# Two attention stages: both heads of a pair turned back to back, weighed values gathered in one PSUM bank

## The chip, the cores and the metric

The kernel runs on one core of a Trainium2 chip, as one program with one launch. The metric is the device time of that program in microseconds, and a version is described by the median of several executions. Abbreviations: PE is TensorE (PEld its weight loads), DVE is VectorE, ACT is ScalarE, POOL is GpSimd, SP is SyncE, which starts most transfers.

## The reference

Two model blocks over a sequence of 2048 rows of width 1024, batch 1, in float32. Only two pieces of them are touched here, the attentions, each with 8 query heads of width 64:

```python
# first block: window of 128 keys to either side, 2 key/value heads, one sink logit per query head
scores = jnp.einsum('bnqhgd,bnkhd->bnhgqk', qb, kb) * (SWA_HEAD_DIM ** -0.5)
scores = jnp.where(valid, scores, -jnp.inf)
mx = jnp.maximum(jnp.max(scores, axis=-1, keepdims=True), sink)
p = jnp.exp(scores - mx)
denom = jnp.sum(p, axis=-1, keepdims=True) + jnp.exp(sink - mx)
out = jnp.einsum('bnhgqk,bnkhd->bnqhgd', p / denom, vb)
...
# second block: chunks of 64 queries, each with its own chunk and the 8 chunks left of it, 8 key/value heads
scores = jnp.where(valid, scores * scale + bias, NEG_BIG)
p = jax.nn.softmax(scores, axis=-1)
out = jnp.einsum('bhcqk,bkhd->bcqhd', p, vb)
```

Around them stand projections, a gated delta rule, a convolution branch, norms and output products. They are not changed.

## The kernel before

The program is a chain of stages, each with its own tiles and semaphores; a stage begins when the one ahead of it has ended. Both attentions are one function, `attention`, called with the name `wa` (window attention, first block) and `ca` (chunk attention, second block). The names of tiles carry this prefix.

**Tiling.** The queries come in 16 tiles of 128 rows. The 8 heads are 4 pairs (m = 0 to 3), the two heads of a pair (g = 0, 1) lie in the upper and the lower 64 partitions. So there are 64 pairs in each attention, two pairs make a half, and a tile has two halves. A query tile sees n key tiles of 128 keys: in `wa` 3 (2 in the first and the last tile), in `ca` 5 (1, 2, 3, 4 in the first four tiles).

**Steps of a pair.**
- Scores (L2013, PE): n key tiles against one query tile, 64 rows deep, the two heads in the two halves of the array at once. Result in `s`, one buffer for each head.
- Maximum (L2131, DVE, for each head): adds bias or mask, negates, takes the row's minimum, writes `neg` (one buffer for each head).
- Exponent (L2192, ACT, for each head): writes `pr` (two rounds of buffers) and the row's sum.
- Turning (L2024, PE, for each head): n transposes of 128x128 with the whole array. Result in `t`, two banks, one buffer that both heads share in turn.
- Copy of what was turned (L2200, ACT, for each head): `t` to `prt`.
- Values (L2038, PE): 2n products with 64 output columns, the two heads in the two column halves of the array. Result in the first half of `o`, one bank for each half of the tile.

**Steps of a half.** Denominators (L2083 with sinks, L2086, L2089, DVE) give `rden`; the spread (L2047, PE) turns it into the second half of the same `o` bank with two whole-array transposes; the copy of the spread (L2211, ACT) brings it to `rd`; finish (L2097, in `ca` also L2103 with the gate, DVE) multiplies the values with it. Once a tile, ACT starts the store (L2216), and in `ca` the load of the gates (L2232).

**Order.** It is written out by hand for each engine. On PE, in the round of pair m: scores(m), turn(m-1, head 0), values(m-2), turn(m-1, head 1), and behind a half's second pair its spread. The array is used in three ways: split by rows (scores), whole (turning, spread), split by columns (values). ACT goes copy(m-1, 0), exponent(m, 0), copy(m-1, 1), exponent(m, 1), with the copy of a spread ahead of the first. DVE goes maximum(m, 0), maximum(m, 1), with finish and denominators behind the second one. Turn(m-1, 1) waits until head 0's turned tile has been copied, since they share `t`. In `wa`, DVE and ACT also split weights for the stage behind it (L2165, L2248) from the eighth tile on.

Of the kernel before, what the change touches and what calls it, by code (L numbers as in the profile page):

```python
# [27 lines left out]
F32 = mybir.dt.float32  # L28
# [7 lines left out]
P = 128  # L36
# [1821 lines left out]
def attention(nc, name, warm, n_warm, consts, load_tile, n_kt, bias_of, bias_shape, load_bias, sink_rows, lanes, shapes, span, out,  # L1858
# [8 lines left out]
    PAIRS = 4  # L1867
    with Ctx(nc, name, USED) as c:
# [6 lines left out]
        neg = [c.sb(f"neg{g}", [P, n_kt * P]) for g in G]  # L1875
        pr = [[c.sb(f"pr{r}{g}", [P, n_kt * P]) for g in G] for r in S]
        prt = [[c.sb(f"prt{r}{g}", [P, n_kt * P]) for g in G] for r in S]
# [7 lines left out]
        s_ps = [c.ps(f"s{g}", [P, bank]) for g in G]  # L1885
        t_ps = c.ps("t", [P, 1024])
        o_ps = [c.ps(f"o{half}", [P, 4, P]) for half in S]
# [3 lines left out]
        scored = c.sems("scored", 2)  # L1891
        max_done = c.sems("max_done", 2)
        exp_done = c.sems("exp_done", 2)
        turned = c.sems("turned", 2)
        pt_copied = c.sems("pt_copied", 2)
        weighed = c.sems("weighed", 2)
# [46 lines left out]
        def program(tile, flush):  # L1943

            for t in range(TILES):
                tile(span_of(t - 1) if t else None, span_of(t))
            flush(span_of(TILES - 1))

        def lagged(before, now, m, lag):

            return (now, m - lag) if m >= lag else (before, m - lag + PAIRS)
# [45 lines left out]
        @block.tensor  # L1997
        def _(pe):
            keep_warm(nc, t_ps[:, 0:NCOL], warm, n_warm)
            pe.wait_ge(const_in, 16 * n_const + START)  # L2000

            def scores(now, m):
                t, u, s, lo, n, b0 = now
                M = PAIRS * t + m
                if m == 0:
                    pe.wait_ge(tile_in, LD * 16 * min(TILES, t + ahead + 1) + START)
                for g in G:
                    wait(pe, max_done[g], M)
                for a in range(0, n * P, 512):
                    w = min(512, n * P - a)  # L2010
                    for g in G:
                        rows = slice(HD * g, HD * g + HD)
                        mm = nc.tensor.matmul(s_ps[g][:, a:a + w], qr[rows, m, t * P:(t + 1) * P],  # L2013
                                              kr[rows, key_tile(m), lo * P + a:lo * P + a + w], start=True, stop=True)
                        if a + w == n * P:
                            mm.then_inc(scored[g], 1)

            def turn(now, m, g):
                t, u, s, lo, n, b0 = now
                M = PAIRS * t + m  # L2020
                pe.wait_ge(exp_done[g], M + 1 + START)
                wait(pe, pt_copied[1 - g], M + g)
                for a in range(n):
                    mm = nc.tensor.transpose(t_ps[:, a * P:(a + 1) * P], pr[m % 2][g][:, a * P:(a + 1) * P], ident[:])  # L2024
                mm.then_inc(turned[g], 1)

            def values(now, m):
                t, u, s, lo, n, b0 = now
                M = PAIRS * t + m
                half = m // 2  # L2030
                for g in G:
                    pe.wait_ge(pt_copied[g], M + 1 + START)
                if m % 2 == 0:
                    wait(pe, half_done[half], t)
                for a in range(n):
                    for g in G:
                        v0 = value_at(m, g)
                        mm = nc.tensor.matmul(o_ps[half][HD * g:HD * g + HD, m % 2, :], vr[:, lo + a, v0:v0 + HD],  # L2038
                                              prt[m % 2][g][:, a * P:(a + 1) * P], start=(a == 0), stop=(a == n - 1))
                        if a == n - 1:  # L2040
                            mm.then_inc(weighed[g], 1)
# [20 lines left out]
            def tile(before, now):  # L2062
                for m in range(PAIRS):
                    scores(now, m)
                    behind(before, now, m)

            def flush(last):
                behind(last, None, 0)
                values(last, PAIRS - 1)
                spread(last, 1)  # L2070

            program(tile, flush)

        @block.vector
        def _(dve):
            def denominators(now, half):
                t, u, s, lo, n, b0 = now
                at = slice(4 * half, 4 * half + 4)
                for g in G:
                    dve.wait_ge(exp_done[g], PAIRS * t + 2 * half + 2 + START)  # L2080
# [11 lines left out]
            def finish(now, half):  # L2092
                t, u, s, lo, n, b0 = now
                dve.wait_ge(rd_copied[half], t + 1 + START)
                if half == 0:
                    wait(dve, stored[s], 16 * u)
                nc.vector.tensor_tensor(ob[s][:, 2 * half:2 * half + 2, :], o_ps[half][:, 0:2, :], rd[half][:],  # L2097
# [11 lines left out]
            def sink_minus_max(now, half):  # L2109
                t, u, s, lo, n, b0 = now  # L2110
                at = slice(4 * half, 4 * half + 4)
                for g in G:
                    dve.wait_ge(max_done[g], PAIRS * t + 2 * half + 2 + START)
# [3 lines left out]
            def tile(before, now):  # L2117
                t, u, s, lo, n, b0 = now
                for m in range(PAIRS):
                    if before is None and not sinks:  # L2120
                        dve.wait_ge(bias_in[m], 16 + START)
                        pair = slice(2 * m, 2 * m + 2)
                        nc.vector.tensor_scalar(bias[:, pair, :], bias[:, pair, :], 1.0 / scale, None, ALU.mult).then_inc(
                            scaled, 1)
                        dve.wait_ge(scaled, m + 1 + START)
                    for g in G:
                        h = 2 * m + g
                        M = PAIRS * t + m
                        dve.wait_ge(scored[g], M + 1 + START)
                        wait(dve, exp_done[g], M)  # L2130
                        nc.vector.tensor_tensor_reduce(neg[g][:, 0:n * P], s_ps[g][:, 0:n * P],  # L2131
                                                       bias_of(bias, h)[:, b0:b0 + n * P], -scale,
                                                       sink[:, 1, h:h + 1] if sinks else HUGE, ALU.add, ALU.min,
                                                       nmx[s][:, h:h + 1]).then_inc(max_done[g], 1)
                        if h == 1 and before:
                            finish(before, 0)
                            denominators(before, 1)
                        if h == 3 and sinks:
                            sink_minus_max(now, 0)
                        if h == 5:  # L2140
                            denominators(now, 0)
                        if merge and t == 13 and h == 2:
                            dve.wait_ge(merge_hi, 1 + START)
                            nc.vector.tensor_tensor(merge.wlo[:], merge.raw[:], merge.whi[:].bitcast(F32),
                                                    ALU.subtract).then_inc(merge_lo, 1)
                        if h == 7 and before:
                            finish(before, 1)
                        if h == 7 and sinks:
                            sink_minus_max(now, 1)
                        if later and t in (2, 3) and h == 4:  # L2150
# [1545 lines left out]
```

## Time and profile before

| | |
|---|---|
| median of 3 runs | 3193.09 us (3183.62 to 3195.11) |
| profiled execution | 3180.22 us, its span 3178.4 us |
| TensorE busy, share of the span | 2981.4 us, 94% |
| VectorE busy | 1791.1 us, 56% |
| ScalarE busy | 1296.3 us, 41% |
| granted TensorE clock, mean | 0.97 |
| `wa`, first turning to last step | 1145.3 to about 1323 us |
| `ca`, first turning to last step | 2555.8 to about 2795 us |

Busy times are of one profiled execution. A matmul's end is modelled, so PE's starts say more than its ends: the distance from the start of one group to the start of the next is what a step costs on PE. In the timeline, rows that belong together are merged (x5 is five instructions), and the brackets at the end give the idle time ahead of a row with what ended it; "issue" means that the profile shows no engine that was waited for.

### The profile page before, as it was taken

To read this page: it belongs to the slowest core of one execution; us is meant where nothing else is said; L and a number is where in the kernel's file an instruction comes from. 1 tells how busy PE (TensorE), PEld (TensorE's weight loads), DVE (VectorE), ACT (ScalarE), POOL (GpSimd) and SP (SyncE) were. 2 spreads that over 40 slices of the span, in tenths; PEclk is the share of its full clock that TensorE was granted. 3 is DMA by queue.
4 is the path that set the end of the run, shared out by engine and by line. 5 is a ranking of instruction groups with operands and counts; after the bars stand their busy time and mean duration, and the time that the engine had idled before them with its cause. 6 is when DMAs were issued, how large, how long until landed. Compare 5 with 4: busy or idle time off the path is not lost. (4 is left out here: it accounts for less than half of the span.)

```text
span 3178.4 us, 56341 instructions
## 1 busy us (share of the span) xinstructions
PE 2981.4 (94%) x21262; PEld 2410.2 (76%) x21262; DVE 1791.1 (56%) x3269; ACT 1296.3 (41%) x2704; POOL 551.5 (17%) x475
## 2 busy tenths in 40 slices
PE   7998999998999989899789999999999989989998
PEld 6886998775888856578468888878888757768787
DVE  5755443074777746655565785565776445553433
ACT  5222433154665558611433323433323367730132
POOL 0000000062343400032022232342233100000000
PEclk9999999999999989999899999999999989999999
DMA  4222775153554432255633223453223263145443
GB/s 140 80 80 75 246 256 195 52 159 134 182 184 151 139 112 94 81 191 186 216 104 106 86 67 103 141 164 107 73 70 106 91 207 115 34 151 213 172 145 119
DMA packets 288037, 423.39 MB, mean 133 GB/s; under 512 B 41520, under 2 KB 178736, under 8 KB 282160
## 3 DMA queue, kind: packets, MB, share of 16 engines
q1 hardware_dynamic: 239312, 383.87, 35.8%
q10 hardware_dynamic: 48480, 36.18, 3.6%
q8 instruction: 162, 2.65, 0.3%
q14 instruction: 83, 0.68, 0.1%
HBM read 270.56 MB, written 149.42 MB: 132 GB/s over the span
## 5 line engine op out<-in xcount | busy, mean ns | idle before, releaser
L114 PE MATMUL pj_pp<-h_hi,pj_whi 128*128 128x512 f32 x1152 | 449.6, 390 | 5.7 <-POOL h_lo L3086 5.7
L116 PE MATMUL pj_pp<-h_hi,pj_wlo 128*128 128x512 f32 x1152 | 448.8, 390 | 0.0
L115 PE MATMUL pj_pp<-h_lo,pj_whi 128*128 128x512 f32 x1152 | 448.7, 389 | 0.0
L114 PEld LDWEIGHTS pj_pp<-h_hi,pj_whi 128*128 128x128 f32 x1152 | 216.4, 188 | 52.1 <-issue 7.6
L2913 ACT CAST pj_whi<-w_raw 128x512 fp32r<-128x512 f32 x192 | 119.5, 624 | 325.6 <-PE pj_pp L116 313.5
L115 PEld LDWEIGHTS pj_pp<-h_lo,pj_whi 128*128 128x128 f32 x1152 | 216.5, 188 | 44.9
L116 PEld LDWEIGHTS pj_pp<-h_hi,pj_wlo 128*128 128x128 f32 x1152 | 216.5, 188 | 44.9
L2977 DVE TENSOR_TENSOR pj_wlo<-w_raw,pj_whi 128x512 fp32r<-128x512 f32 x192 | 161.2, 840 | 12.1 <-ACT pj_whi L2913 8.8
L114 PE MATMUL np_pp<-h_hi,np_whi 128*128 128x512 f32 x384 | 150.4, 392 | 0.0
L115 PE MATMUL np_pp<-h_lo,np_whi 128*128 128x512 f32 x384 | 149.8, 390 | 0.0
L116 PE MATMUL np_pp<-h_hi,np_wlo 128*128 128x512 f32 x384 | 149.7, 390 | 0.0
L2131 DVE CUSTOM_DVE_ANT_0 ca_neg<-ca_s,ca_bias 128x640 f32<-128x640 f32 (+4 forms) x128 | 90.0, 739 | 101.8 <-PE ca_s L2013 100.9
L3106 POOL TENSOR_TENSOR w_raw<-w_raw,pj_t 128x512 f32<-128x512 f32 x48 | 62.7, 1307 | 438.9 <-DVE pj_wlo L2977 438.9
L2913 ACT CAST pj_whi<-pj_t 128x512 fp32r<-128x512 f32 x96 | 59.9, 624 | 173.7 <-PE pj_pp L116 152.2
L1669 POOL TENSOR_TENSOR gr_sw<-gr_tab,gr_wrow 128x64 f32<-128x64 f32 x32 | 15.8, 521 | 642.7 <-DMA gr_ident<-in_consts 642.7
L345 DVE SCALAR_TENSOR_TENSOR np_acc<-np_pre,np_taps,np_acc 128x2048 f32<-128x2048 f32 (+3 forms) x60 | 115.5, 1926 | 2.1
L114 PE MATMUL mo_pp<-ahead_whi,mo_mhi 128*128 128x512 f32 x256 | 103.4, 404 | 0.0
L115 PE MATMUL mo_pp<-ahead_wlo,mo_mhi 128*128 128x512 f32 x256 | 101.8, 398 | 0.0
L116 PE MATMUL mo_pp<-ahead_whi,mo_mlo 128*128 128x512 f32 x256 | 101.8, 397 | 0.0
L2200 ACT COPY ca_prt<-ca_t 128x640 f32<-128x640 f32 (+4 forms) x128 | 80.2, 627 | 51.8 <-PE ca_t L2024 51.2
L114 PE MATMUL fo_pp<-fo_whi,fo_mhi 128*128 128x512 f32 x256 | 99.8, 390 | 0.0
L115 PE MATMUL fo_pp<-fo_wlo,fo_mhi 128*128 128x512 f32 x256 | 99.6, 389 | 0.0
(411 smaller groups left out, 7228.5 us busy)
## 6 DMA issues: line engine op xcount, KB each, us to landing
w_raw<-in_w_second SPq DMA_DIRECT2D x192, 256.0 KB, 2.9
ds_pk<-scratch_pack SPq DMA_DIRECT2D x32, 1280.0 KB, 7.5
scratch_pack<-rp_out SPq DMA_DIRECT2D x32, 512.0 KB, 2.7
scratch_sig_fm<-pj_ob SPq DMA_DIRECT2D x64, 256.0 KB, 2.1
mb_sg<-scratch_sig_fm SPq DMA_DIRECT2D x16, 1024.0 KB, 7.2
rp_fm<-scratch_qkv_fm SPq DMA_DIRECT2D x96, 128.0 KB, 2.9
scratch_qkv_fm<-np_acc SPq DMA_DIRECT2D x11, 1024.0 KB, 4.8
np_acc<-in_x SPq DMA_DIRECT2D x16, 512.0 KB, 4.3
```

What stands on the lines that cost most here:

```text
L114: nc.tensor.matmul(out, ah, bh, start=(first and i == 0), stop=False)
L115: nc.tensor.matmul(out, ah, bl, start=False, stop=False)
L116: mm = nc.tensor.matmul(out, al, bh, start=False, stop=(last and i == n - 1))
L345: nc.vector.scalar_tensor_tensor(out=acc[s][:, at], in0=pre[s][:, at.start + t:at.stop + t], scalar=taps[:, n, t:t + 1], in1=acc[s][:, at] ...
L1669: ins = nc.gpsimd.tensor_tensor(sw[s][:, :, k, a:a + HH], tab[s][:, 1, :, a:a + HH], wrow[:, k, b:b + HH].unsqueeze(1).to_broadcast([P, 2, ...
L2131: nc.vector.tensor_tensor_reduce(neg[g][:, 0:n * P], s_ps[g][:, 0:n * P], bias_of(bias, h)[:, b0:b0 + n * P], -scale, sink[:, 1, h:h + 1] ...
L2200: nc.scalar.copy(prt[m % 2][g][:, 0:n * P], t_ps[:, 0:n * P]).then_inc(pt_copied[g], 1)
L2913: nc.scalar.copy(whi[i], raw_of[i]).then_inc(hi_ready[i], 1)
L2977: nc.vector.tensor_tensor(wlo[i], raw_of[i], whi[i].bitcast(F32), ALU.subtract).then_inc(lo_ready[i], 1)
L3106: nc.gpsimd.tensor_tensor(raw[1][0], raw[1][0], t2[:], ALU.subtract).then_inc(t4_ready, 1)
```

## The change

In both attentions:
- `t` becomes three tiles of one bank each: one for each head, which holds up to four turned key tiles, and a third for the fifth key tile of both heads (`ca` only).
- The two heads of a pair are turned back to back (then, in `ca`, the fifth key tiles of both), and the values of the pair before come behind them. PE's round is scores, spread, turns, values. ACT copies 4 key tiles for each head, and in `ca` with one more instruction the fifth ones of both heads (`copy_last`).
- `o` shrinks to one bank. Values and spread of both halves share it, so there are new waits on PE: the second pair's values of a half wait for the copy of that half's spread (`rd_copied`), and the first pair's values and the spread wait until the other half has been finished (`half_done`). The spread is issued ahead of its half's last values, no longer behind them.
- ACT goes exponent(q, 0), copy of the spread, copy(q-1, 0), exponent(q, 1), copy(q-1, 1), `copy_last`. DVE has finish ahead of the maxima, denominators behind them. The gates' load stands at the head of a tile with a wait of its own, the store one pair earlier.

The new code can take one or two pairs a round (`deep`); both calls pass `deep` = 1, so below SLOTS is (0, 1), GROUPS_OF is 4, NQ is 64, HALF_OF is 2, and q counts pairs.

```diff
-        t_ps = c.ps("t", [P, 1024])
-        o_ps = [c.ps(f"o{half}", [P, 4, P]) for half in S]
+        t_ps = [c.ps(f"t{b}", [P, 4, P]) for b in range(3)]
+        o_ps = c.ps("o", [P, 4, P])
...
+        def half_ending(q):
+
+            return (span_of(q // GROUPS_OF), (q % GROUPS_OF) // HALF_OF) if 0 <= q < NQ and (q + 1) % HALF_OF == 0 else None
...
+            def turns(q):
+                (t, u, s, lo, n, b0), m0 = group(q)
+                for k in SLOTS:
+                    pe.wait_ge(exp_done[k], q + 1 + START)
+                    q1, k1 = bank_before(q, k)
+                    wait(pe, pt_copied[k1], q1 + 1)
+                    for a in range(min(n, 4)):
+                        mm = nc.tensor.transpose(t_ps[bank_of(q, k)][:, a, :], pr[q % 2][k][:, a * P:(a + 1) * P], ident[:])
+                    mm.then_inc(turned[k], 1)
+                if n > 4:
+                    wait(pe, last_copied, last_tiles(q) - 1)
+                    for k in SLOTS:
+                        mm = nc.tensor.transpose(t_ps[2][:, k, :], pr[q % 2][k][:, 4 * P:5 * P], ident[:])
+                    mm.then_inc(last_turned, 1)
+
+            def values(q):
+                (t, u, s, lo, n, b0), m0 = group(q)
+                half = m0 // 2
+                if half_ending(q):
+                    pe.wait_ge(rd_copied[half], t + 1 + START)
+                if m0 % 2 == 0:
+                    wait(pe, half_done[1 - half], t + half)
+                if n > 4:
+                    pe.wait_ge(last_copied, last_tiles(q) + START)
...
             def spread(now, half):
                 t, u, s, lo, n, b0 = now
                 pe.wait_ge(den_inv[half], t + 1 + START)
+                wait(pe, half_done[1 - half], t + half)
                 for r in range(2):
-                    mm = nc.tensor.transpose(o_ps[half][:, 2 + r, :], rden[half][:, r, :], ident[:])
+                    mm = nc.tensor.transpose(o_ps[:, 2 + r, :], rden[half][:, r, :], ident[:])
                 mm.then_inc(spread_done[half], 1)
 
-            def behind(before, now, m):
-                t1, m1 = lagged(before, now, m, 1)
-                t2, m2 = lagged(before, now, m, 2)
-                if t1:
-                    turn(t1, m1, 0)
-                if t2:
-                    values(t2, m2)
-                if t1:
-                    turn(t1, m1, 1)
-                if t2 and m2 % 2:
-                    spread(t2, m2 // 2)
...
+            for q in range(NQ + 2):
+                if q < NQ:
+                    scores(q)
+                if half_ending(q - 2):
+                    spread(*half_ending(q - 2))
+                if 1 <= q <= NQ:
+                    turns(q - 1)
+                if q >= 2:
+                    values(q - 2)
...
             def finish(now, half):
                 t, u, s, lo, n, b0 = now
                 dve.wait_ge(rd_copied[half], t + 1 + START)
+                for k in SLOTS:
+                    dve.wait_ge(weighed[k], (GROUPS_OF * t + HALF_OF * (half + 1)) + START)
...
+            for q in range(NQ + 3):
+                if q < GROUPS_OF and not sinks:
+                    scale_bias(q)
+                if half_ending(q - 3):
+                    finish(*half_ending(q - 3))
+                for k in SLOTS:
+                    if q < NQ:
+                        add_and_max(q, k)
+                    if k == 1 and half_ending(q - 1):
+                        denominators(*half_ending(q - 1))
+                    if q < NQ:
+                        beside(q // GROUPS_OF, 2 * deep * (q % GROUPS_OF) + k)
+                if sinks and half_ending(q):
+                    sink_minus_max(*half_ending(q))
...
+            def copy_last(q):
+                act.wait_ge(last_turned, last_tiles(q) + START)
+                for k in SLOTS:
+                    wait(act, weighed[k], q - 1)
+                nc.scalar.copy(prt[q % 2][:, :, 4 * P:5 * P], t_ps[2][:, 0:2 * deep, :]).then_inc(last_copied, 1)
...
+            for q in range(NQ + 3):
+                if q < NQ and q % GROUPS_OF == 0 and gb is not None:
+                    load_gates(q // GROUPS_OF)
+                for k in SLOTS:
+                    if q < NQ:
+                        exponent(q, k)
+                    if k == 0 and half_ending(q - 2):
+                        copy_spread(*half_ending(q - 2))
+                    if 1 <= q <= NQ:
+                        copy_turned(q - 1, k)
+                    if q < NQ:
+                        beside(q // GROUPS_OF, 2 * deep * (q % GROUPS_OF) + k)
+                if 1 <= q <= NQ and last_tiles(q - 1) > last_tiles(q - 2):
+                    copy_last(q - 1)
+                if sinks and half_ending(q):
+                    sink_exponent(*half_ending(q))
+                if half_ending(q - 3) and half_ending(q - 3)[1]:
+                    store(half_ending(q - 3)[0])
```

## Rows read from the trace of the kernel before

**Rows 1.** Windows: busy time and count by engine, granted clock, DMA share, GB/s.
```profile
1155.00:1320.00 165.00, 162.64 (x1358) 98.68 (x1355) 113.31 (x410) 146.01 (x437) 0.00 (x0) 1.00 0.25 79
2568.00:2792.00 224.00, 223.19 (x2114) 158.25 (x2114) 122.36 (x353) 176.97 (x383) 0.00 (x0) 1.00 0.32 101
...
1148.00:1152.00 4.00, 4.00 (x19) 2.03 (x18) 1.65 (x8) 2.00 (x9) 0.00 (x0) 0.50 0.36 97
...
2561.00:2565.00 4.00, 4.00 (x17) 2.17 (x17) 1.78 (x8) 2.30 (x11) 0.00 (x0) 0.50 0.69 199
```

**Rows 2.** Waits in `ca`, 2555 to 2795: us in total, times, longest.
```profile
DVE ca_neg L2131 <- PE ca_s L2013: 100.9, 61, 2.7
...
PE ca_t L2024 <- ACT ca_prt L2200: 1.1, 2, 0.7
```

**Rows 3.** Timeline of two pairs of `ca`: start, us, engine, line, operation, tiles, shapes, count.
```profile
2699.89 1.35 PE L2013 MATMUL ca_s<-ca_kr,ca_qr 64*128 64x512 f32 x8
...
2700.37 0.83 ACT L2192 ACTIVATE ca_pr<-ca_neg,ca_nmx 128x640 f32<-128x640 f32 x1
...
2701.17 0.76 PE L2024 MATMUL ca_t<-ca_ident,ca_pr 128*128 128x128 f32 x5
2701.19 0.36 ACT L2211 COPY ca_rd<-ca_o 128x256 f32<-128x256 f32 x1
...
2701.87 1.31 PE L2038 MATMUL ca_o<-ca_prt,ca_vr 128*64 128x128 f32 x20
...
2703.11 0.53 PEld L2024 LDWEIGHTS ca_t<-ca_ident,ca_pr 128*128 128x128 f32 x5 [0.17 <-issue]
...
2703.81 1.35 PE L2013 MATMUL ca_s<-ca_kr,ca_qr 64*128 64x512 f32 x8
...
2705.19 0.82 DVE L2131 CUSTOM_DVE_ANT_0 ca_neg<-ca_s,ca_bias 128x640 f32<-128x640 f32 x1 [1.92 <-PE ca_s L2013]
...
2707.02 0.53 PEld L2024 LDWEIGHTS ca_t<-ca_ident,ca_pr 128*128 128x128 f32 x5 [0.17 <-issue]
...
2707.52 0.25 PEld L2047 LDWEIGHTS ca_o<-ca_ident,ca_rden 128*128 128x128 f32 x2
...
2707.94 1.35 PE L2013 MATMUL ca_s<-ca_kr,ca_qr 64*128 64x512 f32 x8
```

**Rows 4.** Timeline of two pairs of `wa`.
```profile
1240.36 0.92 PE L2013 MATMUL wa_s<-wa_kr,wa_qr 64*128 64x384 f32 x4
...
1241.20 0.55 PE L2024 MATMUL wa_t<-wa_ident,wa_pr 128*128 128x128 f32 x3
...
1241.68 0.88 PE L2038 MATMUL wa_o<-wa_prt,wa_vr 128*64 128x128 f32 x12
...
1242.49 0.55 PE L2024 MATMUL wa_t<-wa_ident,wa_pr 128*128 128x128 f32 x3
...
1243.22 0.92 PE L2013 MATMUL wa_s<-wa_kr,wa_qr 64*128 64x384 f32 x4
...
1244.13 0.62 DVE L2131 CUSTOM_DVE_ANT_0 wa_neg<-wa_s,wa_bias,wa_sink 128x384 f32<-128x384 f32 x1 [0.35 <-PE wa_s L2013]
...
1245.20 0.63 ACT L2192 ACTIVATE wa_pr<-wa_neg,wa_nmx 128x384 f32<-128x384 f32 x1
...
1245.91 0.92 PE L2013 MATMUL wa_s<-wa_kr,wa_qr 64*128 64x384 f32 x4
```

**Rows 5.** Timeline at the start of `wa`, where ACT is waiting for a maximum.
```profile
1143.15 0.48 DVE L2131 CUSTOM_DVE_ANT_0 wa_neg<-wa_s,wa_bias,wa_sink 128x256 f32<-128x256 f32 x1 [5.36 <-PE wa_s L2013]
...
1143.74 0.51 ACT L2192 ACTIVATE wa_pr<-wa_neg,wa_nmx 128x256 f32<-128x256 f32 x1 [17.00 <-DVE wa_nmx L2131]
```

**Rows 6.** Timeline at the end of `ca`: last copy, last values, last finish.
```profile
2791.99 0.69 ACT L2200 COPY ca_prt<-ca_t 128x640 f32<-128x640 f32 x1 [1.18 <-PE ca_t L2024]
...
2792.83 1.31 PE L2038 MATMUL ca_o<-ca_prt,ca_vr 128*64 128x128 f32 x20 [0.87 <-ACT ca_prt L2200]
...
2794.95 0.42 DVE L2097 TENSOR_TENSOR ca_ob<-ca_o,ca_rd 128x256 f32<-128x256 f32 x1 [3.19 <-ACT ca_rd L2211]
```

More of the change, by code:

```diff
@@ L1855, in _, with attention @@
             turn(TILES - 1)
-def attention(nc, name, warm, n_warm, consts, load_tile, n_kt, bias_of, bias_shape, load_bias, sink_rows, lanes, shapes, span, out,
+def attention(nc, name, warm, n_warm, consts, load_tile, n_kt, bias_of, bias_shape, load_bias, sink_rows, lanes, shapes, span, deep, out,
               later=None, gate_fm=None, merge=None):
@@ L1867, in attention @@
     PAIRS = 4
+    SLOTS = range(2 * deep)
+    GROUPS_OF = PAIRS // deep
+    NQ = TILES * GROUPS_OF
+    HALF_OF = 2 // deep
+    kp = n_kt * P
     with Ctx(nc, name, USED) as c:
@@ L1884, in attention @@
         bank = 512 if n_kt * P <= 512 else 1024
[L1885 to L1887 removed]
+        s_ps = [c.ps(f"s{k}", [P, bank]) for k in SLOTS]
+        t_ps = [c.ps(f"t{b}", [P, 4, P]) for b in range(3)]
+        o_ps = c.ps("o", [P, 4, P])
         const_in = c.sem("const_in")
@@ L1941, in span_of, with group, bank_of, bank_before @@
             return t, t // 2, t % 2, lo, n, (n_kt - (t + ahead + 1 - lo)) * P
[L1943 to L1951, printed above, removed]
+        def group(q):
+            return span_of(q // GROUPS_OF), deep * (q % GROUPS_OF)
+        def half_ending(q):
+            return (span_of(q // GROUPS_OF), (q % GROUPS_OF) // HALF_OF) if 0 <= q < NQ and (q + 1) % HALF_OF == 0 else None
+        def bank_of(q, k):
+            return k if deep == 1 else (2 * deep * q + k) % 3
+        def bank_before(q, k):
+            return (q - 1, k) if deep == 1 else divmod(2 * deep * q + k - 3, 2 * deep)
+        def last_tiles(q):
+            return max(0, q + 1 - GROUPS_OF * (4 - ahead)) if n_kt > 4 else 0
         @block.sync
@@ L1998, in _, with scores @@
         def _(pe):
-            keep_warm(nc, t_ps[:, 0:NCOL], warm, n_warm)
+            keep_warm(nc, t_ps[0][:].rearrange("p a q -> p (a q)"), warm, n_warm)
             pe.wait_ge(const_in, 16 * n_const + START)
[L2002 to L2005, printed above, removed]
+            def scores(q):
+                (t, u, s, lo, n, b0), m0 = group(q)
+                if m0 == 0:
                     pe.wait_ge(tile_in, LD * 16 * min(TILES, t + ahead + 1) + START)
[L2007 to L2010, printed above, removed]
+                for p in range(deep):
@@ L2011, in scores @@
                     for g in G:
[L2012 to L2035, printed above, removed]
-                    for g in G:
[L2037 to L2041, printed above, removed]
+                        wait(pe, max_done[2 * p + g], q)
@@ new lines, in scores @@
+                    m = m0 + p
+                    for a in range(0, n * P, 512):
+                        w = min(512, n * P - a)
+                        for g in G:
+                            rows = slice(HD * g, HD * g + HD)
+                            mm = nc.tensor.matmul(s_ps[2 * p + g][:, a:a + w], qr[rows, m, t * P:(t + 1) * P],
+                                                  kr[rows, key_tile(m), lo * P + a:lo * P + a + w], start=True, stop=True)
+                            if a + w == n * P:
+                                mm.then_inc(scored[2 * p + g], 1)
@@ L2078, in denominators @@
                 at = slice(4 * half, 4 * half + 4)
-                for g in G:
-                    dve.wait_ge(exp_done[g], PAIRS * t + 2 * half + 2 + START)
+                for k in SLOTS:
+                    dve.wait_ge(exp_done[k], (GROUPS_OF * t + HALF_OF * (half + 1)) + START)
                 if sinks:
@@ L2111, in sink_minus_max @@
                 at = slice(4 * half, 4 * half + 4)
-                for g in G:
-                    dve.wait_ge(max_done[g], PAIRS * t + 2 * half + 2 + START)
+                for k in SLOTS:
+                    dve.wait_ge(max_done[k], (GROUPS_OF * t + HALF_OF * (half + 1)) + START)
                 nc.vector.tensor_tensor(den[s][:, 1, at], nmx[s][:, at], sink[:, 0, at], ALU.add).then_inc(
                     sink_diff[half], 1)
[L2117 to L2150, printed above, removed]
-                            head_squares(t - 2)
-                        if later and t >= 8 and h in (2, 6):
-                            round_off(2 * (t - 8) + h // 4)
@@ new lines, in scale_bias, with add_and_max @@
+            def scale_bias(m):
+                dve.wait_ge(bias_in[m], 16 + START)
+                pair = slice(2 * m, 2 * m + 2)
+                nc.vector.tensor_scalar(bias[:, pair, :], bias[:, pair, :], 1.0 / scale, None, ALU.mult).then_inc(
+                    scaled, 1)
+                dve.wait_ge(scaled, m + 1 + START)
+            def add_and_max(q, k):
+                (t, u, s, lo, n, b0), m0 = group(q)
+                h = 2 * m0 + k
+                dve.wait_ge(scored[k], q + 1 + START)
+                wait(dve, exp_done[k], q)
+                nc.vector.tensor_tensor_reduce(neg[k][:, 0:n * P], s_ps[k][:, 0:n * P],
+                                               bias_of(bias, h)[:, b0:b0 + n * P], -scale,
+                                               sink[:, 1, h:h + 1] if sinks else HUGE, ALU.add, ALU.min,
+                                               nmx[s][:, h:h + 1]).then_inc(max_done[k], 1)
@@ new lines, in beside @@
+            def beside(t, h):
+                if merge and t == 13 and h == 2:
+                    dve.wait_ge(merge_hi, 1 + START)
+                    nc.vector.tensor_tensor(merge.wlo[:], merge.raw[:], merge.whi[:].bitcast(F32),
+                                            ALU.subtract).then_inc(merge_lo, 1)
+                if later and t in (2, 3) and h == 4:
+                    head_squares(t - 2)
+                if later and t >= 8 and h in (2, 6):
+                    round_off(2 * (t - 8) + h // 4)
@@ L2166, in round_off @@
                                         later.piece(later.whi, i).bitcast(F32), ALU.subtract).then_inc(raw_lo, 1)
-            def flush(last):
-                finish(last, 0)
-                denominators(last, 1)
-                finish(last, 1)
             if sinks:
@@ L2210, in copy_spread @@
                 act.wait_ge(spread_done[half], t + 1 + START)
-                nc.scalar.copy(rd[half][:], o_ps[half][:, 2:4, :]).then_inc(rd_copied[half], 1)
+                nc.scalar.copy(rd[half][:], o_ps[:, 2:4, :]).then_inc(rd_copied[half], 1)
             def store(now):
@@ L2217, in store, with load_gates, beside @@
                     stored[s], 16)
-            def tile(before, now):
-                for m in range(PAIRS):
-                    which, mm = lagged(before, now, m, 1)
-                    if m == 0 and before:
-                        copy_spread(before, 0)
-                    if m == 2 and before:
-                        copy_spread(before, 1)
-                    for g in G:
-                        if which:
-                            copy_turned(which, mm, g)
-                        exponent(now, m, g)
-                        if m == 0 and g == 0 and gb is not None:
-                            t, u, s = now[0:3]
-                            act.dma_start(gb[s][:], gate_fm[:, :, t * P:(t + 1) * P].rearrange("m p t -> p m t")).then_inc(
-                                gate_in[s], 16)
-                        if m == 0 and g == 0 and sinks and before:
-                            sink_exponent(before, 1)
-                        if merge and now[0] == 12 and m == 2 and g == 1:
-                            act.wait_ge(merge_w_in, 32 + START)
-                            nc.scalar.copy(merge.whi[:], merge.raw[:]).then_inc(merge_hi, 1)
-                        if m == 2 and g == 0 and sinks:
-                            sink_exponent(now, 0)
-                    if m == 3 and before:
-                        store(before)
-                    if later and 7 <= now[0] < 15 and m in (1, 3):
-                        round_raw(2 * (now[0] - 7) + m // 2)
+            def load_gates(t):
+                s = t % 2
+                wait(act, normed[s], t // 2)
+                act.dma_start(gb[s][:], gate_fm[:, :, t * P:(t + 1) * P].rearrange("m p t -> p m t")).then_inc(gate_in[s], 16)
+            def beside(t, h):
+                if merge and t == 12 and h == 5:
+                    act.wait_ge(merge_w_in, 32 + START)
+                    nc.scalar.copy(merge.whi[:], merge.raw[:]).then_inc(merge_hi, 1)
+                if later and 7 <= t < 15 and h in (3, 7):
+                    round_raw(2 * (t - 7) + h // 4)
             def round_raw(i):
@@ L2248, in round_raw @@
                 nc.scalar.copy(later.piece(later.whi, i), later.piece(later.raw, i)).then_inc(raw_hi, 1)
-            def flush(last):
-                copy_spread(last, 0)
-                for g in G:
-                    copy_turned(last, PAIRS - 1, g)
-                if sinks:
-                    sink_exponent(last, 1)
-                copy_spread(last, 1)
-                store(last)
-                if later:
-                    for s in S:
-                        act.wait_ge(head_eps[s], 1 + START)
-                        nc.scalar.activation(later.st[s][:, 2, :], later.st[s][:, 1, :], ACT.Sqrt).then_inc(head_root, 1)
-            program(tile, flush)
+            for q in range(NQ + 3):
+                if q < NQ and q % GROUPS_OF == 0 and gb is not None:
+                    load_gates(q // GROUPS_OF)
+                for k in SLOTS:
+                    if q < NQ:
[12 more added lines that the diff above has]
+                    store(half_ending(q - 3)[0])
+            if later:
+                for s in S:
+                    act.wait_ge(head_eps[s], 1 + START)
+                    nc.scalar.activation(later.st[s][:, 2, :], later.st[s][:, 1, :], ACT.Sqrt).then_inc(head_root, 1)
 class MixAhead:
```

81 lines of the change are left out of this document (43 added, 38 removed).

## The prediction

> **What bounds the kernel now.** I read the profile in this order. First the windows of the two stages that the change touches [rows 1]: PE is busy 162.64 of 165 us in `wa` and 223.19 of 224 us in `ca`, at the full granted clock, so PE sets the pace of both; ACT is busy for 146.01 of 165 us in `wa`, close behind, and 176.97 of 224 us in `ca`. Then the waits [rows 2]: DVE waits for scores 61 times (100.9 us), PE waits for a copied tile only twice (1.1 us). Nearly everything waits for PE. Last the timelines [rows 3, 4], where the start-to-start distances on PE are to be seen as a round of steps.
>
> In `ca` a pair takes scores 1.28 us (2699.89 to 2701.17), first turning 0.70, values 1.24 (2701.87 to 2703.11), second turning 0.70, in all 3.92 us; a pair with a spread takes 4.13 us (2703.81 to 2707.94), so the spread is 0.21 us, and two pairs take 8.05 us [rows 3]. In `wa`, scores 0.84, turning 0.48, values 0.81 (1241.68 to 1242.49), and two pairs 5.55 us (1240.36 to 1245.91) [rows 4].
>
> **The change, part by part.**
>
> *One tiling change less a pair.* Five transposes and the change behind them take 0.70 us, three take 0.48 us: 0.11 us a transpose and 0.15 for the rest [rows 3, 4]. The weight loads of the second turning, behind values, begin after 0.17 us of idling that no engine caused; the spread's, behind a turning, begin at 2707.52 while the turning's 0.53 us from 2707.02 still run, though a semaphore wait stands ahead of them too [rows 3]. So the gap belongs to the change of tiling and not to the wait. I take 0.17 us a pair; the bounds are nothing (if the second head's two waits bring the gap back) and 0.17. Over 128 pairs: 21.8 us at most. Two turnings back to back are then 0.70 + 0.70 - 0.17 = 1.23 us in `ca` and 0.48 + 0.48 - 0.17 = 0.79 us in `wa`.
>
> *The same transposes, products and copied elements.* Nothing else leaves PE. ACT gets `copy_last`, one instruction more a pair in `ca`: a copy of the spread, the same size, takes 0.36 us [rows 3]. ACT has room for it in `ca` (about 0.8 us of idle a pair by rows 1), and what waits for it is covered: counted from the scores' start, exponent 0 can start at 2.31 us (below), and exponent, copy, exponent, copy at no more than 0.83 and 0.69 each reach 5.4 us, `copy_last` is through by 5.9; PE's next fifth transposes come at 3.75 + 1.28 + 8 x 0.11 = 5.9 us, the values that need it later. If that cover failed it would cost some 0.1 us a pair, 6 us in all.
>
> *The new wait of the values for the spread's copy.* This is the part that decides. In every second round PE has scores(q), spread(q-2), turns(q-1), values(q-2), and these values now wait for `rd_copied`. On ACT the spread's copy is queued behind exponent(q, 0); that waits for maximum(q, 0) on DVE; that waits for scores(q), which PE has just issued. So PE waits for a chain that begins with its own scores of the same round:
> - `ca`: scores' start to maximum 1.38 us (2703.81 to 2705.19) [rows 3]; maximum 0.82, and 0.11 until ACT starts, as at 1143.15 + 0.48 to 1143.74 [rows 5]; exponent to the copy behind it 0.82 (2700.37 to 2701.19) [rows 3]; copy 0.36 [rows 3] and 0.15 until PE starts, as at 2791.99 + 0.69 to 2792.83 [rows 6]. Sum 3.64 us. PE's own way to these values is 1.28 + 0.21 + 1.23 = 2.72 us. It idles for 0.92 us.
> - `wa`: 0.91 (1243.22 to 1244.13) + 0.62 + 0.11 + 0.62 [rows 4] + 0.36 + 0.15 = 2.77 us, against 0.84 + 0.21 + 0.79 = 1.84 us. It idles for 0.93 us.
>
> Queued behind the waiting values on PE are the next scores, so DVE and ACT start late as well, and nothing catches up.
>
> A rule of the Trainium skill bears on this, and it speaks against the change. "PSUM — Partial Sum Buffer", section on bank collisions, says that TensorE may not write a bank while ScalarE reads it, at whatever address, and that the accesses are to be kept apart by semaphores for each bank. By that, putting values and spread of both halves into one bank is what makes this wait necessary. The row gives the same reading of the kernel before: the spread's copy at 2701.19 runs for 0.36 us and the next half's values begin at 2701.87, with no wait of PE for it [rows 2, 3]; there they are in different banks.
>
> *The other new waits* are covered. Finish of a half starts about 0.3 us after its last values and takes 0.42 us [rows 6] (with the gate twice that), while the first values that wait for it stand behind scores and two turnings, 2.5 us in `ca` and 1.6 in `wa`. The spread behind scores waits for denominators made a round earlier. DVE has finish ahead of the maxima now, while PE does scores: 0.3 + 0.9 against 1.38 us in `ca`. The gates' load moves to the head of the tile and the store one round forward, both on ACT's queue, whose copies and exponents do not wait for their landing; SP's and POOL's queues are the same.
>
> *The sum.* `ca`: a round without spread 1.28 + 1.23 + 1.24 = 3.75, with it 3.64 + 1.24 = 4.88, two pairs 8.63 us against 8.05: +0.58, over 32 halves +18.6 us. `wa`: 0.84 + 0.79 + 0.81 = 2.44 and 2.77 + 0.81 = 3.58, two pairs 6.02 us against 5.55: +0.47, over 32 halves +15.0 us. Together +33.6 us. Two corrections. `wa`'s first tile and `ca`'s first two run at the clock of 1.2 GHz [rows 1], where PE's transposes take twice as long: spread, four transposes and change there are 0.44 + 0.88 + 0.17 = 1.5 us behind the scores, and hide most of a chain of about 1.7 us (0.1 + 0.48 + 0.11 + 0.51 + 0.51, rows 3, 5, 6), so that the idle time left is about what two tiling changes save: six halves come out near nothing, where 2 x 0.47 and 4 x 0.58 were counted, -3.3 us. At each stage's end the spread and its copy no longer stand between the last values and finish (2792.83 to 2794.95, 2.12 us [rows 6], becomes about 1.4): -1.4 us. Net +29 us: the profiled execution, 3178.4 us of span and 1.8 us around it, goes from 3180.2 to 3209. The median of the runs shown lies 12.9 us above the profiled one; on it, 3193.1 + 29 = 3222 us, 0.9% slower.
>
> **The rivals.**
> - *The wait is hidden* (the other side). Then only the tiling change is left: up to -21.8 us, 3171 us on the median; in `wa` ACT takes over before all of it is had. Its rounds are 4 x 0.62 + 4 x about 0.4 + 0.4 for spread and sinks + 0.5 for the split weights = 5.0 us of the 5.1 that PE would need, which leaves room for stalls, so -12 is as likely. It decides when the chain is shorter than PE's own way, 2.72 and 1.84 us. For it: PE never waited for `rd` before. Against it: the chain is 0.9 us longer than that, and its first two links are fixed by the scores.
> - *Partly hidden*: a quarter to a half of the idle time (59 us over 64 halves) is covered by slack that I overlook: 29 less 15 to 30, so about 0 to +14 us, 3193 to 3207.
> - *The gap is the semaphore's, not the tiling's.* Then nothing is saved, and the idle time stays (0.17 less each, since PE's way is longer): 29 + 21.8 - 64 x 0.17 = +40 us, 3233. The spread's gapless start speaks against it [rows 3].
> - *The clock falls.* In a round with a spread PE would have 0.21 + 1.1 us of transposes and 0.9 us of idling between two groups of products. At 1.2 GHz in both stages PE's 386 us would come near to twice that: up to +386 us, 3580. Against it: with transposes in a third of PE's time both stages ran at 1.00, and half speed shows only in their first tiles [rows 1]. The Trainium skill, "TensorE: Matmul & The Clock Gate", part 4 on transposes, says that transposes do not count as activity for the clock in the way products do; by that rule this rival is what to fear. The full clock of rows 1, with turning in every pair, bears it out only in so far as products lie between.
>
> **How the numbers follow.** My forecast 0.78, hidden wait 0.07, partly hidden 0.07, gap of the semaphore 0.06, clock 0.02. The predicted time is the forecast's, 3222 us. Its own range is 3212 to 3234: the idle time by 0.15 us either way (64 halves, 10 us). The range takes in part of the cases beside it and the width of the runs shown (11.5 us): 3206 to 3240. A measurement of this kernel can tell about 0.5%, 16 us. Faster by over that is only the hidden wait at its best, 0.04; within it the rest of that and the partly hidden case, 0.10; slower 0.86.
>
> **What would show it in the profile after.** Waits of PE (or of its weight loads) at the values for ACT's spread copy, 32 times in each attention and about 0.9 us each, some 55 us in all; none of size elsewhere on PE. Turnings of both heads with no gap between them. Rounds of 3.75 and 4.88 us in `ca`, 2.44 and 3.58 us in `wa`. `wa` and `ca` longer by 13 and 16 us, all other stages the same. ACT idle ahead of exponent 0 until the maximum. The prediction is wrong if the values after a spread start less than 2.9 us (`ca`) or 2.0 us (`wa`) behind their scores, or if other stages move.

## The result and the profile after

| | before | after |
|---|---|---|
| median of 12 runs | 3184.55 us (3176.37 to 3195.11) | 3200.51 us (3191.69 to 3213.09) |
| ratio, 95% interval | | 1.0054 [1.0042, 1.0066] |
| span of the profiled execution | 3178.4 us | 3199.0 us |
| `wa`, first to last scores | 1141.7 to 1317.2: 175.5 us | 1145.9 to 1329.4: 183.5 us |
| `ca`, first to last scores | 2549.7 to 2785.4: 235.7 us | 2559.2 to 2804.8: 245.6 us |

The change costs 0.5%, 13 to 21 us. Slower was forecast, but 3222 us and the range from 3206 us lie above 3200.51. In the two executions the attentions account for 16.4 us: 8.0 and 9.9 us between the first and the last scores, and 1.5 us given back behind these. The rest of the 20.6 us between the spans, 4.2 us, lies in stages that are the same code. It is no more than the spread between executions: the first scores of `wa` come 4.2 us later already, and in the six further kernels below, whose code ahead of them is that of the changed kernel, they come at 1143.4 to 1149.5 us.

Timeline of the kernel after, a round of `ca` without and one with a spread (it answers to [rows 3]):

```profile
2723.61 1.35 PE L2031 MATMUL ca_s<-ca_kr,ca_qr 64*128 64x512 f32 x8
...
2724.89 0.86 PEld L2043 LDWEIGHTS ca_t<-ca_ident,ca_pr 128*128 128x128 f32 x8
...
2726.13 1.07 PEld L2067 LDWEIGHTS ca_o<-ca_prt,ca_vr 128*64 128x64 f32 x20 [0.17 <-issue]
...
2727.38 1.35 PE L2031 MATMUL ca_s<-ca_kr,ca_qr 64*128 64x512 f32 x8
...
2728.66 0.44 PE L2077 MATMUL ca_o<-ca_ident,ca_rden 128*128 128x128 f32 x2
2728.76 0.82 DVE L2147 CUSTOM_DVE_ANT_0 ca_neg<-ca_s,ca_bias 128x640 f32<-128x640 f32 x1 [1.77 <-PE ca_s L2031]
...
2729.62 0.83 ACT L2207 ACTIVATE ca_pr<-ca_neg,ca_nmx 128x640 f32<-128x640 f32 x1 [0.80 <-DVE ca_nmx L2147]
...
2730.45 0.35 ACT L2233 COPY ca_rd<-ca_o 128x256 f32<-128x256 f32 x1
...
2730.86 0.33 PE L2067 MATMUL ca_o<-ca_prt,ca_vr 128*64 128x128 f32 x2 [0.67 <-ACT ca_rd L2233]
...
2732.10 1.35 PE L2031 MATMUL ca_s<-ca_kr,ca_qr 64*128 64x512 f32 x8
```

The chain can be read downwards from 2727.38: scores, 1.38 us later the maximum, 0.86 us later the exponent, 0.83 us later the spread's copy, 0.41 us later the values, which waited for it. The round without a spread takes 3.77 us, the one with it 4.72 us, and the eight transposes of both heads begin with no gap inside.

The same round in `wa` (it answers to [rows 4]):

```profile
1253.93 0.92 PE L2031 MATMUL wa_s<-wa_kr,wa_qr 64*128 64x384 f32 x4
...
1254.88 0.62 DVE L2147 CUSTOM_DVE_ANT_0 wa_neg<-wa_s,wa_bias,wa_sink 128x384 f32<-128x384 f32 x1 [0.68 <-PE wa_s L2031]
...
1255.54 0.62 ACT L2207 ACTIVATE wa_pr<-wa_neg,wa_nmx 128x384 f32<-128x384 f32 x1 [0.41 <-DVE wa_nmx L2147]
...
1256.15 0.35 ACT L2233 COPY wa_rd<-wa_o 128x256 f32<-128x256 f32 x1
...
1256.56 0.88 PE L2067 MATMUL wa_o<-wa_prt,wa_vr 128*64 128x128 f32 x12 [0.69 <-ACT wa_rd L2233]
...
1257.36 0.92 PE L2031 MATMUL wa_s<-wa_kr,wa_qr 64*128 64x384 f32 x4
```

Waits of the kernel after, in `wa` (1145 to 1340 us) and in `ca` (2559 to 2815 us), as in [rows 2]: total, times, longest:

```profile
PE wa_o L2067 <- ACT wa_rd L2233: 21.4, 32, 0.7
...
PE ca_o L2067 <- ACT ca_rd L2233: 19.8, 31, 0.7
```

PE waits once for each half, 63 times, 41.2 us; before there is no such row. Windows of the kernel after, to be held against the first two of [rows 1]:

```profile
1155.00:1325.00 170.00, 148.91 (x1315) 95.97 (x1312) 109.29 (x393) 136.92 (x422) 0.00 (x0) 1.00 0.25 79
2575.00:2810.00 235.00, 215.48 (x2098) 158.68 (x2098) 124.31 (x353) 172.65 (x430) 0.00 (x0) 1.00 0.31 98
```

PE has about 20 us of idling in each stage, at the full clock.

### The profile page after: what moved, and what is told of

The parts are those of the page before. It is cut to its first block and busy times, and to the rows that moved or that the text cites. A ratio compares the mean times of both kernels' runs of the same rounds, so it can differ in the third digit from the quotient of the medians.

```text
span 3199.0 us, 56614 instructions
## 1 busy us (share of the span) xinstructions
PE 2959.4 (93%) x21241; PEld 2414.1 (75%) x21262; DVE 1786.4 (56%) x3269; ACT 1283.2 (40%) x2752; POOL 551.4 (17%) x475
## 5 line engine op out<-in xcount | busy, mean ns | idle before, releaser
L2207 ACT ACTIVATE ca_pr<-ca_neg,ca_nmx 128x640 f32<-128x640 f32 (+4 forms) x128 | 97.7, 764 | 68.8 <-DVE ca_nmx L2147 68.8
L116 PE MATMUL fo_pp<-fo_whi,fo_mlo 128*128 128x512 f32 x256 | 99.6, 389 | 0.0
```

What stands on the lines that cost most here:

```text
L116: mm = nc.tensor.matmul(out, al, bh, start=False, stop=(last and i == n - 1))
L2207: nc.scalar.activation(pr[q % 2][k][:, 0:n * P], neg[k][:, 0:n * P], ACT.Exp, bias=nmx[s][:, h:h + 1], scale=-1.0, accum_out=den[s][:, 0, ...
```

## The experiments

A is the theory of the prediction: PE waits for the spread's copy, since ACT has it behind an exponent that depends on the round's own scores. Rival B: the new order on ACT and DVE is itself slower, and the wait only shows it. The first experiment and the last two have 4 to 6 executions, the others one each; of those the lengths in the trace are used. Lengths below are those between first and last scores in `wa` and `ca`; the changed kernel has 183.5 and 245.6 us.

**The spread's copy first.** One move on ACT:

```diff
                 for k in SLOTS:
+                    if k == 0 and half_ending(q - 2):
+                        copy_spread(*half_ending(q - 2))
                     if q < NQ:
                         exponent(q, k)
-                    if k == 0 and half_ending(q - 2):
-                        copy_spread(*half_ending(q - 2))
```

> On ACT the spread's copy is moved ahead of exponent(q, 0), so it no longer waits for the round's own scores and maximum; nothing else changes. Theory A (the loss is PE's wait for the spread's copy, whose chain begins with the scores of the same round): the copy is done 1.28 + 0.48 + 0.41 = 2.2 us behind the scores' start in `ca` and 0.84 + 0.48 + 0.41 = 1.7 us in `wa`, ahead of PE's own way to the values (2.75 and 1.87 us), so no wait is left there. First to last scores go from 183.5 to about 164 us in `wa` (two pairs 5.26 us) and from 245.6 to about 225 us in `ca` (two pairs 7.74 us); against the kernel before about -24 us, ratio 0.9925. Theory B (the loss is made by the new order of exponents and copies on ACT and of finish on DVE, and the wait for the spread only shows where PE would wait anyway): the wait moves to another instruction, both stages stay within 3 us of the changed kernel, ratio about 1.005.

Measured: 164.0 and 225.6 us, median 3155.97 us, ratio to the kernel before 0.9906 [0.9878, 0.9935]. Timeline of this kernel in `ca`, a round with a spread:

```profile
2684.99 1.35 PE L2031 MATMUL ca_s<-ca_kr,ca_qr 64*128 64x512 f32 x8
...
2686.27 0.44 PE L2077 MATMUL ca_o<-ca_ident,ca_rden 128*128 128x128 f32 x2
2686.37 0.83 DVE L2147 CUSTOM_DVE_ANT_0 ca_neg<-ca_s,ca_bias 128x640 f32<-128x640 f32 x1 [1.77 <-PE ca_s L2031]
...
2686.74 0.37 ACT L2233 COPY ca_rd<-ca_o 128x256 f32<-128x256 f32 x1 [0.31 <-PE ca_o L2077]
...
2687.24 0.83 ACT L2207 ACTIVATE ca_pr<-ca_neg,ca_nmx 128x640 f32<-128x640 f32 x1
...
2687.72 1.07 PEld L2067 LDWEIGHTS ca_o<-ca_prt,ca_vr 128*64 128x64 f32 x20 [0.17 <-issue]
```

The copy runs while PE is still turning; what is left ahead of the values is the tiling change. (In `wa` the profile puts this remainder down to the copy: weight loads wait for it 31 times, 5.9 us in all, 0.19 us each.) The exponent starts 0.87 us behind the start of its maximum, against 0.86 us in the changed kernel: it loses nothing to the copy, since ACT was idle then. B falls as the cause of the loss: but for this one copy the order on ACT, and all of DVE's, is that of the changed kernel, and the loss is gone. The mended kernel is some 0.9% faster than the kernel before. Its median is 29 us lower where 24 were expected; the spans of the two traces differ by 24.4 us, of which 23.5 lie in the two stages, and the rest is spread.

**The spread's copy later.** The opposite move, behind `copy_turned(q - 1, 0)`:

> The changed kernel with the spread's copy one place later on ACT, behind copy_turned(q-1, 0): the suspected chain is made longer by one copy, 0.49 us in `ca` and 0.38 us in `wa`, 32 times each. Theory A: PE's wait at the values grows by just that, `wa` by about 11 us (to 195) and `ca` by about 14 us (to 260) from first to last scores, in all +25 us against the changed kernel. Theory B: that copy is not on the path, less than 5 us in all.

Measured: 194.9 and 257.8 us, 3228.47 us in one run. Waits of this kernel in `wa`:

```profile
PEld wa_o L2067 <- ACT wa_rd L2233: 40.5, 32, 1.3
...
PE wa_o L2067 <- ACT wa_rd L2233: 32.9, 32, 1.1
```

And in `ca`:

```profile
PE ca_o L2067 <- ACT ca_rd L2233: 34.4, 32, 1.2
```

`wa` grows by 11.4 us and its wait by 32.9 - 21.4 = 11.5 us, 0.36 us for each half. In `ca` the wait grows by 14.6 us, and the steady rounds with a spread go from 4.72 to 5.21 us; the stage grows only by 12.2 us, since its first two tiles take 0.7 us less than in the changed kernel's trace and the last half's wait lies behind the last scores. In the steady rounds this chain is paid in full: the time of the copy put in front is what PE waits longer.

**A bank for the spread in `wa`.** The tiles of `wa` take 6 banks (two for `s`, three for `t`, one for `o`), those of `ca` 8, since there each `s` takes two. So in `wa` the spread can have a seventh:

```diff
+        own = n_kt <= 4
+        r_ps = c.ps("r", [P, 4, P]) if own else o_ps
...
-                if half_ending(q):
+                if half_ending(q) and not own:
                     pe.wait_ge(rd_copied[half], t + 1 + START)
...
-                    mm = nc.tensor.transpose(o_ps[:, 2 + r, :], rden[half][:, r, :], ident[:])
+                    mm = nc.tensor.transpose(r_ps[:, 2 + r, :], rden[half][:, r, :], ident[:])
...
-                nc.scalar.copy(rd[half][:], o_ps[:, 2:4, :]).then_inc(rd_copied[half], 1)
+                nc.scalar.copy(rd[half][:], r_ps[:, 2:4, :]).then_inc(rd_copied[half], 1)
```

> In `wa` alone, where a bank is free, the spread gets a bank of its own, and the second pair's values of a half no longer wait for the spread's copy; ACT's and DVE's orders are those of the changed kernel, `ca` is as in the changed kernel. Theory A (shared bank, hence the wait): `wa` loses its waits for the copy and goes from 183.5 to about 169 us between first and last scores, `ca` stays at 245.6 us. Theory B: `wa` stays within 3 us of 183.5.

Measured: 166.4 and 244.1 us, 3181.37 us in one run. In `wa` no row shows PE waiting for the spread's copy any more; in `ca` it still stands:

```profile
PE ca_o L2069 <- ACT ca_rd L2235: 19.6, 31, 0.7
```

`wa` loses 17.1 us with ACT's order untouched. So it is the one shared bank that makes the wait, and ACT's order that makes it long; removing either takes nearly all of it away. Of rival B some 2 us may be left: `wa` takes 166.4 us here and 164.0 us in the first experiment, and the rounds without a spread take 2.65 us here against 2.46 us there, up to the eighth tile. That this is ACT's order is likely and not tested.

**The old turning in half of the rounds.**

```diff
+                if 2 <= q <= NQ and not half_ending(q - 2):
+                    turns(q - 1, range(0, 1))
+                    values(q - 2)
+                    turns(q - 1, range(1, 2))
+                    continue
                 if 1 <= q <= NQ:
                     turns(q - 1)
```

> The kernel of the first experiment, but in the rounds without a spread (32 in each attention) PE goes turn(q-1, head 0), values(q-2), turn(q-1, head 1) again: one tiling change more in 64 rounds, same instructions, same waits for the other engines. Theory A (a tiling change costs 0.17 us of PE, whatever semaphore waits stand there): 64 x 0.17 = +10.9 us against the first experiment, about +5.4 in each attention. Rival (the gap belongs to the semaphore waits, which are the same in both): within 2 us of the first experiment.

Measured: 169.3 and 229.1 us, +5.3 and +3.5 us, 3169.83 us in one run. Timeline of this kernel in `ca`, one of those rounds:

```profile
2690.81 1.35 PE L2031 MATMUL ca_s<-ca_kr,ca_qr 64*128 64x512 f32 x8
...
2692.68 1.31 PE L2067 MATMUL ca_o<-ca_prt,ca_vr 128*64 128x128 f32 x20
...
2693.92 0.42 PEld L2043 LDWEIGHTS ca_t<-ca_ident,ca_pr 128*128 128x128 f32 x4 [0.17 <-issue]
...
2694.73 1.35 PE L2031 MATMUL ca_s<-ca_kr,ca_qr 64*128 64x512 f32 x8
```

It takes 3.92 us, as before the change [rows 3], against 3.77 us: a tiling change is 0.15 us, 64 of them 9.6 us by the rounds and 8.8 by the stages. The gap is not the semaphores', which are the same. The two numbers for the stages are less sure than the rounds: in the first tiles, where PE also waits for transfers and for DVE, the two traces differ by +1.6 us in `wa` and -1.2 us in `ca`. Behind them the stages grow by 3.7 and 4.6 us, where 30 rounds of 0.15 us are 4.5; in `wa` some rounds are bound by another wait and stay as they were.

**Two pairs at once in `wa`** (`deep` = 2 in its call, with the spread's copy first):

> The first experiment's kernel with `deep` = 2 in `wa`: two pairs are scored, turned and weighed together, three tiling changes for two pairs instead of six; `ca` as in the first experiment. If tiling changes at 0.17 us each are what PE still loses in `wa`: 3 x 0.17 us less for two pairs, from 5.32 to about 4.8 us, where ACT's own work (4 exponents at 0.61, 4 copies at 0.37, 0.26 for the spread, 0.1 for sinks, 0.5 for a split) takes over at about 4.8 us: `wa` goes from 164.0 to 150 to 156 us between first and last scores. Rival: with three banks for four turned tiles and a single score buffer a head, PE waits for ACT inside the group, and `wa` stays at 160 us or more.

Measured: 162.1 us where 150 to 156 were expected, ratio to the kernel before 0.9928 [0.9905, 0.9951], not to be told from the first experiment's. The expectation missed, the rival holds. Waits of this kernel in `wa`:

```profile
ACT wa_rd L2233 <- PE wa_o L2077: 23.6, 31, 1.9
...
PE wa_t L2043 <- ACT wa_prt L2215: 16.8, 31, 0.8
```

PE waits once a group for a copy, 16.8 us, which is about what three tiling changes less in each of 32 groups save (32 x 3 x 0.15 = 14.4 us). In the timeline that wait stands ahead of the fourth head's transposes, whose bank is the first head's:

```profile
1253.83 0.37 ACT L2233 COPY wa_rd<-wa_o 128x256 f32<-128x256 f32 x1 [0.47 <-PE wa_o L2077]
...
1254.10 0.62 ACT L2207 ACTIVATE wa_pr<-wa_neg,wa_nmx 128x384 f32<-128x384 f32 x1
...
1254.71 0.47 ACT L2215 COPY wa_prt<-wa_t 128x384 f32<-128x384 f32 x1
...
1255.32 0.52 PE L2043 MATMUL wa_t<-wa_ident,wa_pr 128*128 128x128 f32 x3 [0.55 <-ACT wa_prt L2215]
```

It is the same kind of chain again: ACT waits for the spread that PE issues in this very round, does the spread's copy and an exponent, and only then the copy that PE needs. That another place for the spread's copy would shorten it here was not tried.

**The split of weights behind the maxima in `wa`** (`h in (3, 7)` for `h in (2, 6)` ahead of `round_off` on DVE, on top of the first experiment):

> The first experiment's kernel, and in `wa` from the ninth tile on the split of weights on DVE (L2172 in that kernel, 0.69 us) stands behind the pair's second maximum instead of between the two. In the first experiment's trace the scores behind a round with a split start 0.17 us late, since they wait for that second maximum. If that is what is left there: 16 such rounds by 0.17 us, about -2.5 us in `wa` (164.0 to 161.5 us between first and last scores), `ca` unchanged. Rival: the exponent and the next round's first maximum come late instead, no change.

Measured: 161.9 us, as expected, ratio to the kernel before 0.9929 [0.9902, 0.9956]. The rounds with a spread from the ninth tile on go from 2.86 to 2.68 us, which is the 0.17 us expected. A gain of 2 us that only the trace can show.

## Why the prediction missed its range

Its mechanism was right step by step. The tiling change: 0.17 us taken, 0.15 measured. The wait: at the values, for the spread's copy, once a half, nowhere else of size on PE; about 0.7 us each and 41 us in all, where 0.9 and 55 were named. Rounds without spread: 3.75 and 2.44 us forecast, 3.77 (2723.61 to 2727.38) and 2.45 us measured. The other new waits and `copy_last` cost nothing that shows. Of the rivals, "the wait is hidden" is what the first experiment turned the kernel into, at -0.9% where it was given -0.4 to -0.7%. By its time alone the result lies in the stretch of another, "partly hidden" (3193 to 3207 us, chance 0.07). But that is not what happened: no slack covers the wait, the values start 0.06 us behind the end of the copy, and the wait is shorter because its chain is.

The step that failed is the size of one term, the chain of the new wait, "Sum 3.64 us" in `ca` and 2.77 us in `wa`. Measured are 3.48 and 2.63 us, 0.16 and 0.14 less:

| link | taken, `ca` / `wa` | measured |
|---|---|---|
| scores' start to maximum | 1.38 / 0.91 | 1.38 / 0.95 |
| maximum to exponent | 0.93 / 0.73 | 0.86 / 0.66 |
| exponent to copy | 0.82 / 0.62 | 0.83 / 0.61 |
| copy to values | 0.51 / 0.51 | 0.41 / 0.41 |

Both links that are off by more than 0.04 us are handoffs between engines, each taken from one row at the edge of a stage. [Rows 5] is the very first exponent of the stage; there, 0.11 us pass between the maximum's end and the exponent, in a steady round 0.04. [Rows 6] is the last copy of a stage, 0.15 us ahead of PE, against 0.06 us for the spread's copy. With the rounds without a spread, two pairs come to 8.49 and 5.88 us instead of 8.63 and 6.02: +0.44 and +0.33, 32 times each +24.6 us where +33.6 were counted. That is 9.0 of the 12.5 us between the forecast +29 and the 16.4 us of the two traces.

The second correction, -1.4 us for the stages' ends, came out at -1.5. The first, for the tiles at half speed, took 3.3 us off; measured is more. From the first scores to those of the second tile, `wa` went from 12.7 to 10.6 us and `ca` from 12.1 to 10.2 us, 4.1 us less than before, where the same count of rounds had put +1.5: 5.6 us off. In the further kernels, one trace each, these first tiles take 9.8 to 11.5 us (`wa`, the five with one pair a round) and 9.6 to 10.7 us (`ca`, all six), so it is no accident of the changed kernel's one trace; of the kernel before there is only one. Two things are seen to go into it. The new order spares a wait: before, the second head of the first pair of `wa` was turned 0.55 us late, since it waited for the first head's copy. And the clock rose earlier, as windows at the start of `wa` show, the first of the kernel before, the second of the kernel after:

```profile
1153.00:1157.00 4.00, 4.00 (x22) 2.01 (x20) 0.86 (x4) 1.78 (x8) 0.00 (x0) 0.56 0.35 98
...
1153.00:1157.00 4.00, 3.34 (x30) 2.19 (x29) 1.65 (x8) 2.98 (x12) 0.00 (x0) 0.93 0.37 99
```

PE ran at 1.2 GHz until 14.7 us behind the first scores of `wa` before (to 1156.5 us), until 7.6 us behind them after (to 1153.5 us), and until 7.5 to 11.1 us in the six further kernels. How the 5.6 us divide between the two, and why the clock rose earlier, no run tells.

What is left, about -1 us, is a sum of parts with both signs, the largest of which are these. The second tiles grow by 0.1 us in all where 1.5 were counted (-1.4), and the last tiles, part of whose last half lies behind the last scores, by 0.35 instead of 1.5 (-1.2). Against them stands a misreading in the prediction. Its 5.55 us for two pairs of `wa` come from the ninth tile on, where DVE and ACT also split weights [rows 4]; in the tiles ahead of these two pairs took 5.43 us, as here in the kernel before:

```profile
1196.51 0.92 PE L2013 MATMUL wa_s<-wa_kr,wa_qr 64*128 64x384 f32 x4
...
1199.34 0.92 PE L2013 MATMUL wa_s<-wa_kr,wa_qr 64*128 64x384 f32 x4
...
1201.94 0.92 PE L2013 MATMUL wa_s<-wa_kr,wa_qr 64*128 64x384 f32 x4
```

The kernel after takes 5.89 us in both parts, so the third to the eighth tile of `wa` lost 5.6 us instead of the 4.0 that +0.33 a half makes (+1.6).

The range missed for one more reason: it stood on the median of 3193.1 us of three runs. Twelve runs of the same kernel have 3184.55 us. Of the 21.5 us between forecast and result, 8.5 are this. It and the chain's 9.0 us are of one size, and either of them put right alone would have moved the range down far enough to hold 3200.5 us.

## What to carry to other kernels

When two results are moved into one PSUM bank, the price is in the wait that keeps them apart: follow it back through every queue, and see whether the chain begins with work that the waiting engine has just issued. Then only the engine's own work on the way can hide it (here 2.75 of 3.48 us), and a late start of one engine carries over to the others. Reorder the queue in the middle (one moved copy was worth 1.4% here, 3200.5 to 3156.0 us; by the traces 39.5 us between first and last scores) before giving up the layout. A wait repeated 64 times turns a handoff misread by 0.07 us into 4.5 us, so take handoffs from steady rows, or give them both bounds. A round's length too is to be read in each part of a stage that does other work beside it. And a forecast in absolute time should hold the spread of the reference's median too.

## What the runs showed of the hardware

PE idling for 0.7 us in every second round, with 1.3 us of transposes ahead of it, did not lower the granted clock: 1.00, the level of 2.4 GHz, in both windows of the kernel after. The Trainium skill, "TensorE: Matmul & The Clock Gate", part 4, says that transposes don't count as activity for the clock in the way products do; no run here tests it, since products stand between them in every round. A change of how the array is split took 0.15 us of PE more a round (3.92 against 3.77 us in `ca`, 2.61 against 2.46 us in `wa`), with the same waits and products. A handoff from one engine to another was no constant: 0.04 us from DVE to ACT in steady rounds of the kernel after and 0.11 us at the first exponent of `wa` before [rows 5]; 0.06 us from ACT's copy of 256 columns to PE in the kernel after, 0.15 us from one of 640 columns at the end of `ca` before [rows 6].
